# Attention probabilities turned by VectorE and SyncE's transfers, in place of TensorE

## The chip, the cores and the metric

The kernel runs on one core of a Trainium2 chip. The metric is the device time of one execution in microseconds (us). A core has TensorE (matrix products), VectorE, ScalarE and GpSimd, and SyncE, which here only issues transfers (DMA) and waits. Data lies in SBUF (128 partitions), products land in the eight banks of PSUM. In rows of the profile PE is a matmul, PEld its weight load, DVE VectorE, ACT ScalarE, POOL GpSimd, SPq SyncE's queue. L1409 is line 1409 of the kernel.

## The reference

Two different transformer blocks, one after the other, on a batch of 1, 512 tokens of width 1024, in f32. The first is attention over a sliding window (8 heads of 64, 2 key heads) beside a gated convolution, and a feed-forward part of width 2816. The second is two hybrid layers, each with a chunked attention (8 heads of 64) and a retention (4 heads of 128). What the change touches is the two attentions:

```python
def sliding_window_attention(q, k, v, sinks):      # first block: 128 queries, 256 keys
    scores = jnp.einsum("bnqhgd,bnkhd->bnhgqk", q, kw).astype(jnp.float32) * ATTN_SCALE
    scores = jnp.where(mask[None, :, None, None], scores, -jnp.inf)
    probs = jax.nn.softmax(jnp.concatenate([scores, sink], axis=-1), axis=-1)[..., :-1]
    out = jnp.einsum("bnhgqk,bnkhd->bnqhgd", probs.astype(v.dtype), vw)

def chunked_rel_attention(q, k, v, rel_bias):      # second block, both layers
    scores = jnp.einsum("bnqhd,bnkhd->bnhqk", qc, kb) * (dh ** -0.5)
    scores = jnp.where(valid, scores + bias[None, None], NEG_INF)
    p = jax.nn.softmax(scores, axis=-1)
    out = jnp.einsum("bnhqk,bnkhd->bnqhd", p, vb)
```

## The kernel before

**Units and projections.** All weights are taken in units of 1024 x 128. Two units are a panel, which SyncE loads into one of two slots of `raw` (two transfers of 512 KB) once `lo_ready` says that the units before it in this slot are split: panel n waits for 2n - 2 units. For unit u, ScalarE rounds it to `w_hi` and VectorE writes the rest, `w_lo`; both do so for unit u + 4 after TensorE's unit u. TensorE then takes 8 steps of three products (hi x hi, hi x lo, lo x hi, L608 to L610), 512 tokens wide, into one bank of `main`, and VectorE empties the bank with `apply_factor` (`bank_empty`). Numbers of units run through the whole program: 0 to 33 the first block's input, 50 to 93 the up projection, from 116 the second block's two layers with 40 units each.

**Attention in rounds and slots.** A round is two heads' scores for one or two blocks of 128 queries, 384 or 512 score columns in each of two banks (`half`). The first block has 8 rounds (four of them with 384 columns), each layer of the second has 10 (all 512). Rounds are threaded into the projection of other tiles in slots. Slot r lies after so many steps of the projection: in the first block in the middle of unit 20 + r, in the layers every 6 steps (`ATT2_SLOTS`). In slot r, in the order of each engine's queue:

- TensorE turns the probabilities of round r - 2 with transposes of 128 x 128 against `ident` (L687, six or eight a round) into `aux[2]` and `main[3]`, then makes the scores of round r (L698) in `aux[0]` and `aux[1]`, and in every second slot from r = 4 the value products of rounds r - 4 and r - 3 (`mix`, L675) in `aux[3]`.
- VectorE divides the exponentials of round r - 1 by their sums (`normalise`: reciprocal L1481, scaling L1486), takes scores plus table and maximum of round r out of the banks (`soften`, L1458), and reads `aux[3]` after value products.
- ScalarE copies the turned banks to SBUF (`copy_turned`, L1083) and takes the exponentials of round r (L1073), in the first block with one small exponential for each sink (L1070).

On VectorE and ScalarE a slot stands ahead of the unit's own work, `apply_factor` and split. All queues are in order, so work behind a slot waits for it. While the attention runs, the projection uses three banks of `main`. In the second block's layer 0 VectorE also scales `h` in units 6 to 13 of the layer, and from unit 17 on ScalarE, VectorE and GpSimd make the rotary tiles (`swapped`, `straight`).

**The start.** x arrives in four chunks and is turned on TensorE; the first four units are multiplied together, step by step as x comes. Their two panels are loaded by halves (4 of 8 rows of tiles each), and a unit's first product waits for `w_lo` of its first half. Twenty transposes of `ident` stand ahead (`warm_up`).

**The up projection's start.** In units 42 to 49 (out projection) ScalarE and VectorE split u + 4 ahead of adding the residual and rounding x. After unit 50 TensorE sums squares for the norm (`sum_norm`, L634), after unit 51 it spreads the factor.

Of the kernel before, what the change touches and what calls it, by code (L numbers as in the profile page):

```python
# [31 lines left out]
P = 128  # L32
# [41 lines left out]
ATT1 = 20  # L74
# [67 lines left out]
def two_blocks_kernel(  # L142
# [31 lines left out]
    diag_hi = keep("diag_hi", [P, NB, P], F32R)  # L174
    sum_sq_at = placed[0]
# [4 lines left out]
    squares = keep("squares", [P, 2, SEQ], F32)  # L180
    taps = keep("taps", [P, 132], F32)
# [42 lines left out]
    soft1_half = at("soft1_half", [P, 2, SEQ], F32, 88)  # L224
    turned1_pair = at("turned1_pair", [P, 2, 2, SEQ], F32, 80)
# [20 lines left out]
    soft2_pair = at("soft2_pair", [P, 2, 2, SEQ], F32, 80)  # L246
    turned2_half = at("turned2_half", [P, 2, SEQ], F32, 88)
# [19 lines left out]
    def soft1(r, half):  # L267
        return squares[:, half, :] if r % 2 else soft1_half[:, half, :]

    def soft2(r, half):  # L270
        return soft2_pair[:, r % 2, half, :]

    def turned1(r):
        return sum_sq if r % 3 == 2 else turned1_pair[:, r % 3, :, :]

    def turned2(r):
        return (turned2_half, squares, sum_sq)[r % 3]
# [17 lines left out]
    turned_banks = (aux[2], main[3])  # L295
# [32 lines left out]
    half_loaded = [sem("half_loaded0"), sem("half_loaded1")]  # L328
# [14 lines left out]
    bank_empty = sem("bank_empty")  # L343
    ident_ready = sem("ident_ready")
# [29 lines left out]
    probs_ready = sem("probs_ready")  # L374
    probs_turned = sem("probs_turned")
    turned_ready = sem("turned_ready")
# [96 lines left out]

    def in_rows(u):
        return u >= ROWS or u >= IN2 and (u - IN2) % LAYER_UNITS < VALUE_UNITS
# [14 lines left out]
    def _(sp):  # L490
        def panel(n, first, second):

            if n >= 2:
                sp.wait_ge(lo_ready, 2 * n - 2)
            load(n % 2, first, second)
# [30 lines left out]
        def first_panel(i, half):  # L526
            rows = tile_rows(w_in[0], 4 * half, 4, IN1_TILES[2 * i] * P, 256)
            sp.dma_start(raw[:, i, 4 * half:4 * half + 4, :], rows)\
                .then_inc(raw_loaded[i] if half else half_loaded[i], 16)
# [7 lines left out]
        x_chunk(2)  # L537
        x_chunk(3)
# [33 lines left out]
        def rows_panel(n, w, pair, column):  # L572
            sp.wait_ge(lo_ready, 2 * n - 2)
# [27 lines left out]
    def _(pe):  # L601
# [63 lines left out]
        def mix(n, spans, value, turned):  # L665

            pe.wait_ge(turned_ready, n + 1)
            if n >= 2:
                pe.wait_ge(mixed_read, n - n % 2)
            for step, (t, b, blocks, columns) in enumerate(spans):  # L670
                for j, kb in enumerate(blocks):
                    for half in range(2):
                        rows = slice(64 * half, 64 * half + 64)
                        column = columns.start + j * P
# [5 lines left out]
        def turn(n, r, spans, soft):  # L680

            if n >= 1:
                pe.wait_ge(turned_ready, n)
            for half in range(2):
                pe.wait_ge(probs_ready, 2 * n + half + 1)
                for j in range(spans[-1][3].stop // P):
                    done = pe.transpose(block_of(turned_banks[half], j), block_of(soft(r, half), j), ident[:])  # L687
                done.then_inc(probs_turned, 1)

        def score(n, spans, queries, keys):  # L690
            for t, b, blocks, columns in spans:
                query = queries[:, t, b * P:(b + 1) * P]
                key = keys(t)[:, blocks[0] * P:(blocks[-1] + 1) * P]
                for half in range(2):
                    if n >= 1 and columns.start == 0:
                        pe.wait_ge(peaked, 2 * n - 1 + half)
                    rows = slice(64 * half, 64 * half + 64)
                    done = pe.matmul(aux[half][:, columns], query[rows], key[rows], start=True, stop=True)  # L698
# [37 lines left out]
        def first_products(u, k):  # L736
            pe.wait_ge(x_ready, k + 1)
            if k == 0:
                pe.wait_ge(half_lo, u + 1)
# [1299 lines left out]
```

## Time and profile before

| | |
|---|---|
| time, median of 3 runs (lowest to highest) | 1218.19 us (1217.56 to 1218.64) |
| profiled execution: its own time / its span | 1218.59 us / 1216.7 us |
| TensorE busy (matmuls) | 1206.9 us, 5966 instructions |
| TensorE weight loads | 990.8 us |
| VectorE busy | 708.9 us, 1264 |
| ScalarE busy | 535.2 us, 948 |
| GpSimd busy | 90.5 us, 79 |
| granted clock, mean | 0.999 of full speed |
| moved by transfers | 114.05 MB, mean 94 GB/s |

Busy time of TensorE is from the start of a matmul to its modelled end, and neighbouring matmuls overlap. The span runs from the first to the last instruction of the profile; the execution's own time is 1.9 us longer. Durations come from this one execution.

### The profile page before, as it was taken

The page shows a single profiled execution, that of the slowest core. Times are in us where ns is not written, and L with a number is a line of the kernel's source. Part 1 is how long each engine was busy: PE and PEld are TensorE (multiplying, and loading weights), DVE is VectorE, ACT ScalarE, POOL GpSimd, SP SyncE. Part 2 cuts the span into 40 slices and gives each one's busy share as a digit, 9 for nine tenths or more (in the row PEclk, how much of TensorE's full clock was granted, in tenths as well). Part 3 has the DMA queues.
Part 4 walks back from the last instruction along what each step waited for, and adds up shares of the span by engine and source line. Part 5 has one row for each costly group of instructions (what it writes and reads, how often), then busy time and mean ns, then how long its engine had stood idle before and what let it go on. Part 6 is the DMA issues. An engine that isn't in the chain of part 4 may idle for free.

```text
span 1216.7 us, 16176 instructions
## 1 busy us (share of the span) xinstructions
PE 1206.9 (99%) x5966; PEld 990.8 (81%) x5966; DVE 708.9 (58%) x1264; ACT 535.2 (44%) x948; POOL 90.5 (7%) x79
## 2 busy tenths in 40 slices
PE   8999999999999999999999999999999999999997
PEld 7888788888888888888888887788888887788886
DVE  5555665564577777775642546665555335665654
ACT  4522563444444344442242424554654325454653
POOL 3000000002100000000010200033002000043000
PEclk9999999999999999999999999999999999999999
DMA  6333222332233223322233432222223521222121
GB/s 213 106 104 104 70 70 70 104 102 82 94 103 103 77 96 103 103 103 89 94 104 104 177 101 69 71 69 70 70 69 104 173 76 64 70 69 70 70 87 70
DMA packets 98202, 114.05 MB, mean 94 GB/s; under 512 B 3801, under 2 KB 82875, under 8 KB 98011
## 3 DMA queue, kind: packets, MB, share of 16 engines
q1 hardware_dynamic: 95755, 107.69, 27.0%
q10 hardware_dynamic: 2384, 5.51, 1.2%
q8 instruction: 41, 0.67, 0.2%
q14 instruction: 22, 0.18, 0.0%
HBM read 111.05 MB, written 2.14 MB: 93 GB/s over the span
## 4 chain that ended last, share of the span: by engine, by line
PE 97%; DVE 1%; DMA 1%; ACT 1%; issue 0%; POOL 0%; SPq 0%; ACTq 0%; DVEq 0%; POOLq 0%
PE main L608 23%; PE main L610 23%; PE main L609 23%; PE aux L608 3%; PE aux L610 3%; PE aux L609 3%; PE main L926 2%; PE main L928 2%; PE main L927 2%; PE aux L698 2%; PE aux L675 2%; PE aux L687 1%; PE main L687 1%; DMA raw<-in_w_in_dram 1%; PE main L993 1%; PE main L992 1%
## 5 line engine op out<-in xcount | busy, mean ns | idle before, releaser
L1409 DVE TENSOR_TENSOR w_lo<-raw,w_hi 128x1024 fp32r<-128x1024 f32 x192 | 243.6, 1270 | 266.3 <-ACT w_hi L1035 262.2
L608 PE MATMUL main<-x_hi,w_hi 128*128 128x512 f32 x984 | 392.1, 398 | 1.4 <-DVE w_lo L1496 1.4
L610 PE MATMUL main<-x_hi,w_lo 128*128 128x512 f32 x984 | 383.7, 390 | 0.0
L609 PE MATMUL main<-x_lo,w_hi 128*128 128x512 f32 x984 | 383.6, 390 | 0.0
L1035 ACT ACTIVATE w_hi<-raw 128x1024 fp32r<-128x1024 f32 x192 | 202.4, 1055 | 262.6 <-PE main L610 161.2
L608 PEld LDWEIGHTS main<-x_hi,w_hi 128*128 128x128 f32 x984 | 184.8, 188 | 50.6 <-issue 14.3
L610 PEld LDWEIGHTS main<-x_hi,w_lo 128*128 128x128 f32 x984 | 184.7, 188 | 39.6
L609 PEld LDWEIGHTS main<-x_lo,w_hi 128*128 128x128 f32 x984 | 185.0, 188 | 35.8
L1073 ACT ACTIVATE soft_pair<-soft_pair,neg_peak 128x128 f32<-128x128 f32 (+2 forms) x64 | 35.3, 553 | 56.3 <-DVE neg_peak L1465 56.3
L1446 DVE TENSOR_TENSOR up_in<-main,factor 128x512 f32<-128x512 f32 x44 | 30.4, 690 | 37.8 <-PE main L610 34.8
L926 PE MATMUL main<-w_hi,x_hi 128*128 128x512 f32 x128 | 50.5, 394 | 0.0
L928 PE MATMUL main<-w_lo,x_hi 128*128 128x512 f32 x128 | 50.0, 390 | 0.0
L927 PE MATMUL main<-w_hi,x_lo 128*128 128x512 f32 x128 | 49.9, 390 | 0.0
L1980 POOL COPY sum_sq<-squares 128x512 f32<-128x512 f32 x4 | 2.7, 670 | 618.4 <-ACT squares L1052 618.4
L1983 POOL TENSOR_TENSOR sum_sq<-sum_sq,squares 128x512 f32<-128x512 f32 x28 | 37.7, 1345 | 116.1 <-ACT squares L1052 115.4
L2001 POOL TENSOR_TENSOR swapped_pair<-swapped_pair,sin_t 128x512 f32<-128x512 f32 x16 | 24.4, 1528 | 256.7 <-ACT swapped_pair L1331 256.7
L1205 ACT ACTIVATE g_hi<-squares 128x512 f32 (+1 forms) x22 | 13.9, 633 | 65.1 <-DVE squares L1654 65.1
L608 PE MATMUL aux<-g_hi,w_hi 128*128 128x512 f32 x88 | 34.2, 389 | 0.0
L609 PE MATMUL aux<-g_lo,w_hi 128*128 128x512 f32 x88 | 34.2, 389 | 0.0
L610 PE MATMUL aux<-g_hi,w_lo 128*128 128x512 f32 x88 | 34.2, 389 | 0.0
L608 PE MATMUL main<-g_hi,w_hi 128*128 128x512 f32 x88 | 34.2, 389 | 0.0
L609 PE MATMUL main<-g_lo,w_hi 128*128 128x512 f32 x88 | 34.2, 389 | 0.0
(281 smaller groups left out, 1810.7 us busy)
## 6 DMA issues: line engine op xcount, KB each, us to landing
raw<-in_w_in_dram SPq DMA_DIRECT2D x98, 512.0 KB, 4.4
raw<-in_w_up_dram SPq DMA_DIRECT2D x44, 512.0 KB, 3.9
raw<-in_w_out_dram SPq DMA_DIRECT2D x24, 512.0 KB, 4.1
raw<-in_w_down_dram SPq DMA_DIRECT2D x22, 512.0 KB, 4.1
rel<-band_rows ACTq DMA_DIRECT2D x2, 2048.0 KB, 9.7
x_rows<-in_x_dram SPq DMA_DIRECT2D x4, 512.0 KB, 8.5
raw<-in_w_attn_branch_dram SPq DMA_DIRECT2D x4, 512.0 KB, 3.4
raw<-in_w_conv_branch_dram SPq DMA_DIRECT2D x4, 512.0 KB, 4.3
```

The source lines that it names most:

```text
L608: pe.matmul(bank, hi, right_hi[j], start=first and j == 0, stop=False)
L609: pe.matmul(bank, hi, right_lo[j], start=False, stop=False)
L610: done = pe.matmul(bank, lo, right_hi[j], start=False, stop=last and j == len(rows) - 1)
L926: pe.matmul(bank, x, hi, start=k == 0, stop=False)
L927: pe.matmul(bank, rest, hi, start=False, stop=False)
L928: return pe.matmul(bank, x, lo, start=False, stop=k == KT - 1)
L1035: act.activation(w_hi[:, u % 4, :, :], raw_unit(u), ACT.Copy).then_inc(hi_ready, 1)
L1073: done = act.activation(block, block, ACT.Exp, bias=neg_peak[which], accum_out=total[which])
L1409: dve.tensor_tensor(w_lo[:, u % 4, :, :], raw_unit(u), w_hi[:, u % 4, :, :].bitcast(F32), ALU.subtract).then_inc(lo_ready, 1)
L1446: dve.tensor_tensor(target, all_banks[main_bank(u)][:], factor[:], ALU.mult).then_inc(bank_empty, 1)
L1983: pool.tensor_tensor(sum_sq[:, 0, :], sum_sq[:, 0, :], tile, ALU.add)\
L2001: steps.then(pool.tensor_tensor(swapped(n), swapped(n), sin_t[:], ALU.mult))
```

## The change

**Attention.** TensorE's transposes (`turn`) and ScalarE's copies (`copy_turned`) go. VectorE transposes each round's probabilities by blocks of 32 x 32 into `blocks_turned`, one instruction for each half, and 16 transfers on SyncE's queue move the blocks of two rounds to where the whole is turned (each 32 partitions x 2 rounds x 256 columns, 64 KB). `normalise` moves from VectorE to ScalarE; VectorE keeps the reciprocal (`find_shares`). For the sinks VectorE subtracts the maxima for a round in one instruction and ScalarE takes one exponential. Work of two rounds now shares a slot: scores in even slots r for rounds r and r + 1, shares and normalising in slot r + 1, turning in slot r + 2, value products in slot r + 4. Two pairs of banks alternate for scores, so that `aux[2]` and `main[3]` hold scores too. `ATT1_SLOTS` and `ATT2_SLOTS` give the new places in steps: from unit 19.5 with 18 steps for two slots, and from 11.5 of each layer with 13 steps for two slots (6 more from slot 4). A move stands in SyncE's queue ahead of the first panel n for which the unit of its slot r + 2 is below 2n - 6. In a layer ScalarE waits ahead of the first rotary tile for `mixed`, GpSimd ahead of the fifth for the last `probs_turned`, since buffers share space.

**The start.** The first panels are loaded and split in pieces of 2, 2 and 4 rows. Step 0 of the four units goes two units at a time, product by product, each with a wait for its own operand. Five products of `mean` and seven transposes of `ident` replace most of the warm-up.

**The up projection.** The splits of units 52 and 53 go behind the residual and the rounding of x, the sum of the norm and the spreading go two steps into units 51 and 52.

```diff
+ATT1_SLOTS = [156 + 18 * (r // 2) + 10 * (r % 2) for r in range(len(ROUNDS1) + 3)]
-ATT2_SLOTS = [92 + 6 * r for r in range(len(ROUNDS2) + 3)]
+ATT2_SLOTS = [92 + 13 * (r // 2) + 8 * (r % 2) + (6 if r >= 4 else 0) for r in range(len(ROUNDS2) + 3)]
-ATT1 = 20
+ATT1 = 19
...
+    def rounds_scored(r, rounds):
+        return (r, r + 1) if r % 2 == 0 and r < len(rounds) else ()
+    def rounds_turned(r, rounds):
+        return (r - 2, r - 1) if r % 2 == 0 and 2 <= r < len(rounds) + 2 else ()
...
+    def round_banks(n):
+        return (aux[2], main[3]) if n % 2 else (aux[0], aux[1])
...
+        def move_blocks(n, turned):
+            sp.wait_ge(probs_turned, 2 * n + 4)
+            if n >= 4:
+                sp.wait_ge(mixed, n - 2)
+            for a in range(4):
+                for b in range(4):
+                    sp.dma_start(turned[32 * b:32 * b + 32, :, 256 * a:256 * a + 256],
+                                 blocks_turned[32 * a:32 * a + 32, :, b, :])\
+                        .then_inc(turned_ready[n // 2 % 2], 16)
+
+        def moves_before(n):
+            while moves and moves[0][0] < 2 * n - 6:
+                unit, r, turned = moves.pop(0)
+                move_blocks(r, turned)
...
         def mix(n, spans, value, turned):
-            pe.wait_ge(turned_ready, n + 1)
+            groups = turned[:, n % 2, :].rearrange("p (a s) -> p a s", a=4)
+            pe.wait_ge(turned_ready[n // 2 % 2], turned_count(n))
...
-                                         turned[:, half, column:column + P],
+                                         groups[:, :, at:at + 32],
...
+        def first_step(u):
+            hi, lo = w_hi[:, u % 4, 0, :], w_lo[:, u % 4, 0, :]
+            pe.wait_ge(x_hi_ready, 1)
+            pe.wait_ge(half_hi, u + 1)
+            pe.matmul(main[u][:], hi, x_hi[:, 0, :], start=True, stop=False)
+            yield
+            pe.wait_ge(x_ready, 1)
+            pe.matmul(main[u][:], hi, x_lo[:, 0, :], start=False, stop=False)
+            yield
+            pe.wait_ge(half_lo, u + 1)
+            pe.matmul(main[u][:], lo, x_hi[:, 0, :], start=False, stop=False)
+            yield
...
         for u in range(UP, UP + 4):
-            project(u, 1, wait=u == UP)
-            if u == UP:
-                sum_norm(2 * KT)
-            if u == UP + 1:
-                spread_factor(1)
+            def between(k, u=u):
+                if k == 2 and u == UP + 1:
+                    sum_norm(2 * KT)
+                if k == 2 and u == UP + 2:
+                    spread_factor(1)
+            project(u, 1, between, wait=u == UP)
...
+        def normalise(n, r, spans, soft):
+            act.wait_ge(shares_ready, n + 1)
             for half in range(2):
-                act.wait_ge(probs_turned, 2 * n + half + 1)
-                done = act.activation(turned[:, half, 0:width], turned_banks[half][:, 0:width], ACT.Copy)
-            done.then_inc(turned_ready, 1)
+                for step, (t, b, blocks, columns) in enumerate(spans):
+                    block = soft(r, half)[:, columns]
+                    done = act.activation(block, block, ACT.Copy, scale=share[:, n % 2, half, step:step + 1])
+                done.then_inc(probs_ready, 1)
...
+        def attention_slot(r, first, rounds, soft, sinks):
+            for m in rounds_scored(r, rounds):
+                exps(first + m, m, rounds[m], soft, sinks)
+            for m in rounds_scored(r - 1, rounds):
+                normalise(first + m, m, rounds[m], soft)
...
+        def turn(n, r, spans, soft):
+            if n >= 2:
+                before = n - n % 2 - 2
+                dve.wait_ge(turned_ready[before // 2 % 2], turned_count(before))
...
             for half in range(2):
+                dve.wait_ge(probs_ready, 2 * n + half + 1)
+                places = blocks_turned[:, r % 2, :, P * half:P * half + width // 4]
+                dve.transpose(places.rearrange("p b (k i) -> p k b i", i=32),
+                              soft(r, half)[:, 0:width].rearrange("p (k b j) -> p k b j", b=4, j=32))\
+                    .then_inc(probs_turned, 1)
...
         def slot1(r):
+            for m in rounds_scored(r - 1, rounds1):
+                find_shares(m, rounds1[m], True)
+            for m in rounds_turned(r, rounds1):
+                turn(m, m, rounds1[m], soft1)
+            for m in rounds_scored(r, rounds1):
+                soften(m, m, rounds1[m], lambda t, b, half: window[:, 0 if b else P:256], 0.125,
                        lambda t, half: sink_cols[:, 2 * t + half:2 * t + half + 1], soft1)
+                subtract_from_sinks(m, rounds1[m])
             for m in rounds_mixed(r, rounds1):
                 read_mixed(m, mixed_tile(q1, ROUNDS1[m]))
...
+                    if i == 17:
+                        act.wait_ge(mixed, len(ROUNDS1) + len(ROUNDS2) * layer + 4)
...
+                if n % 8 == 4:
+                    pool.wait_ge(probs_turned, 2 * (len(ROUNDS1) + len(ROUNDS2) * (layer + 1)))
```

## Rows read from the trace of the kernel before

**Rows 1.** The page, part 1: busy us, share of the span, instructions of each engine

```profile
PE 1206.9 (99%) x5966; PEld 990.8 (81%) x5966; DVE 708.9 (58%) x1264; ACT 535.2 (44%) x948; POOL 90.5 (7%) x79
```

**Rows 2.** TensorE's waits: us in total, times, longest us

```profile
PE main L608 <- DVE w_lo L1496: 1.4, 1, 1.4
PE aux L634 <- POOL sum_sq L1983: 0.2, 1, 0.2
```

**Rows 3.** Busy time by window: PE, PEld, VectorE, ScalarE, GpSimd; clock, DMA share, GB/s

```profile
736.00:826.00 90.00, 90.00 (x565) 69.91 (x564) 57.26 (x165) 45.89 (x106) 13.33 (x9) 1.00 0.18 59
```

**Rows 4.** TensorE's timeline: start us, us, instruction, at slots with scores and turning

```profile
126.34 0.93 PE L698 MATMUL aux<-k_twice,q 64*128 64x128 f32 x8
...
741.39 0.39 PE L609 MATMUL main<-x_lo,w_hi 128*128 128x512 f32 x1
741.61 0.39 PE L610 MATMUL main<-x_hi,w_lo 128*128 128x512 f32 x1
741.93 1.13 PE L698 MATMUL aux<-k,q 64*128 64x512 f32 x4
...
743.33 0.39 PE L609 MATMUL main<-x_lo,w_hi 128*128 128x512 f32 x1
...
753.25 0.39 PE L610 MATMUL main<-x_hi,w_lo 128*128 128x512 f32 x1
...
755.85 0.39 PE L609 MATMUL main<-x_lo,w_hi 128*128 128x512 f32 x1
```

**Rows 5.** The chain that ended last: start us, us, scores and value products

```profile
742.00 1.06 PE aux L698 x4
...
761.83 1.90 PE aux L675 x32
```

**Rows 6.** Groups of TensorE: busy us, mean ns of one, idle before

```profile
L675 PE MATMUL aux<-sum_sq,v 128*64 128x128 f32 x96 | 6.5, 277 | 0.0
```

**Rows 7.** TensorE's timeline at the start of the kernel

```profile
7.77 0.47 PE L608 MATMUL main<-x_hi,w_hi 128*128 128x512 f32 x1
...
10.80 0.47 PE L608 MATMUL main<-x_hi,w_hi 128*128 128x512 f32 x1 [1.43 <-DVE w_lo L1496]
```

**Rows 8.** ScalarE's timeline at the start of the kernel

```profile
9.30 1.15 ACT L1095 ACTIVATE w_hi<-raw 128x512 fp32r<-128x512 f32 x2 [1.54 <-DMA raw<-in_w_in_dram]
```

**Rows 9.** Groups of VectorE, shapes apart

```profile
L1458 DVE CUSTOM_DVE_ANT_0 soft_pair<-aux,rel 128x512 f32<-128x512 f32 x16 | 10.4, 686 | 1.4 <-PE aux L698 1.4
...
L1486 DVE TENSOR_SCALAR soft_pair<-soft_pair,share 128x512 f32<-128x512 f32 x16 | 7.1, 484 | 0.3
```

**Rows 10.** Groups of ScalarE, shapes apart

```profile
L1039 ACT ACTIVATE x_hi<-h,cols 128x512 fp32r<-128x512 f32 x16 | 11.6, 725 | 31.8 <-DVE h L1624 31.8
```

**Rows 11.** SyncE's timeline, small loads at the start

```profile
10.68 0.36 SPq L513 DMA_DIRECT2D vec_rows<-in_final_norm_dram  x1
...
13.40 0.42 SPq L523 DMA_DIRECT2D consts<-shape_constants  x1
```

**Rows 12.** Issues of transfers: count, KB each, median us from issue to landing

```profile
raw<-in_w_in_dram SPq DMA_DIRECT2D x98, 512.0 KB, 4.4
...
out_dram<-out_rows SPq DMA_DIRECT2D x8, 256.0 KB, 2.2
```

**Rows 13.** VectorE's timeline, first block and second block's layer 0

```profile
126.92 0.68 DVE L1446 TENSOR_TENSOR gates<-main,factor 128x512 f32<-128x512 f32 x1
...
755.99 0.17 DVE L1481 RECIPROCAL share<-total 128x4 f32<-128x4 f32 x1
...
761.89 1.23 DVE L1409 TENSOR_TENSOR w_lo<-raw,w_hi 128x1024 fp32r<-128x1024 f32 x1 [2.38 <-ACT w_hi L1035]
...
763.70 0.17 DVE L1481 RECIPROCAL share<-total 128x4 f32<-128x4 f32 x1
```

**Rows 14.** ScalarE's timeline, second block's layer 0

```profile
758.83 0.51 ACT L1073 ACTIVATE soft_pair<-soft_pair,neg_peak 128x256 f32<-128x256 f32 x1 [3.57 <-DVE neg_peak L1465]
...
760.82 1.04 ACT L1035 ACTIVATE w_hi<-raw 128x1024 fp32r<-128x1024 f32 x1
```

More of the change, by code:

```diff
@@ L490, in _ @@
     def _(sp):
+        moves = [(ATT1_SLOTS[r + 2] / 8, r, turned1(r // 2)) for r in range(0, len(ROUNDS1), 2)]
+        for layer in range(LAYERS):
+            moves += [(IN2 + LAYER_UNITS * layer + ATT2_SLOTS[r + 2] / 8,
+                       len(ROUNDS1) + len(ROUNDS2) * layer + r, turned2(r // 2)) for r in range(0, len(ROUNDS2), 2)]
+        def move_blocks(n, turned):
[11 more added lines that the diff above has]
+                move_blocks(r, turned)
         def panel(n, first, second):
+            moves_before(n)
             if n >= 2:
@@ L673, in mix @@
                         rows = slice(64 * half, 64 * half + 64)
-                        column = columns.start + j * P
+                        at = P * half + columns.start // 4 + 32 * j
                         done = pe.matmul(aux[3][rows, mixed_columns(n, step)], value(t, kb, half),
-                                         turned[:, half, column:column + P],
+                                         groups[:, :, at:at + 32],
                                          start=j == 0, stop=j == len(blocks) - 1)
             done.then_inc(mixed, 1)
[L680 to L688, printed above, removed]
         def score(n, spans, queries, keys):
@@ L694, in score, with attention_slot @@
                 for half in range(2):
-                    if n >= 1 and columns.start == 0:
-                        pe.wait_ge(peaked, 2 * n - 1 + half)
+                    if n >= 2 and columns.start == 0:
+                        pe.wait_ge(peaked, 2 * (n - 2) + half + 1)
                     rows = slice(64 * half, 64 * half + 64)
-                    done = pe.matmul(aux[half][:, columns], query[rows], key[rows], start=True, stop=True)
+                    done = pe.matmul(round_banks(n)[half][:, columns], query[rows], key[rows], start=True, stop=True)
                     if columns == spans[-1][3]:
                         done.then_inc(scored, 1)
-        def attention_slot(r, first, rounds, queries, keys, value, soft, turned):
-            if 2 <= r < len(rounds) + 2:
-                turn(first + r - 2, r - 2, rounds[r - 2], soft)
-            if r < len(rounds):
-                score(first + r, rounds[r], queries, keys)
+        def attention_slot(r, first, rounds, queries, keys, value, turned):
+            for m in rounds_scored(r, rounds):
+                score(first + m, rounds[m], queries, keys)
             for m in rounds_mixed(r, rounds):
-                mix(first + m, rounds[m], value, turned(m))
-        pe.wait_ge(ident_ready, 1)
+                mix(first + m, rounds[m], value, turned(m // 2))
+        pe.wait_ge(mean_ready, 1)
         def warm_up(times):
@@ L717, in warm_up @@
                 pe.transpose(main[3][:, 0:P], ident[:], ident[:])
-        warm_up(3)
+        for _ in range(5):
+            pe.matmul(main[3][:, 0:P], mean[:], mean[:], start=True, stop=True)
+        pe.wait_ge(ident_ready, 1)
         pe.wait_ge(mix_loaded, 16)
@@ L747, in _ @@
         turn_x(1)
-        warm_up(12)
-        for k in range(KT - 2):
+        warm_up(7)
+        for pair in ((0, 1), (2, 3)):
+            for _ in zip(*[first_step(u) for u in pair]):
+                pass
+        turn_x(2)
+        for k in range(1, KT - 2):
             for u in range(FIRST_UNITS):
                 first_products(u, k)
-                if u == (3 if k == 0 else 1):
+                if u == 1:
                     turn_x(k + 2)
@@ L844, in slot2 @@
                 for t in range(4):
-                    if r < len(ROUNDS2) and t in [step[0] for step in ROUNDS2[r]]:
+                    if t in [step[0] for m in rounds_scored(r, ROUNDS2) for step in ROUNDS2[m]]:
                         pe.wait_ge(bank_empty, emptied(u0 + KEY_UNITS[t]))
@@ L1598, in _ @@
                 convolve(t, t % 2)
-            if u - ATT1 in (4, 6, 8, 10):
-                attn_rest((u - ATT1 - 4) // 2)
+            for t in range(4):
+                if 8 * u < ATT1_SLOTS[2 * t + 4] <= 8 * u + 8:
+                    attn_rest(t)
         def merged_rest(m):
```

207 lines of the change are left out of this document (117 added, 90 removed).

## The prediction

> **What bounds the kernel now.** I read the page first. TensorE is busy for 1206.9 of 1216.7 us [rows 1]. The view of TensorE's waits names only short ones, 1.4 us for the first split weights and 0.2 us for a sum on GpSimd [rows 2]. So a microsecond taken out of TensorE's queue is a microsecond of the end, as long as nothing comes late to TensorE. The rest is about that condition: in the attention windows VectorE is busy for 57.3 of 90 us and ScalarE for 45.9 [rows 3], and I walked the timelines of both, and of SyncE, to see whether they can follow.
>
> **What leaves TensorE.** In its timeline products follow each other every 0.22 to 0.23 us: a step (three products) is 0.68 us, a unit of 24 products 5.44. A slot with scores alone takes 743.33 - 741.61 = 1.72 us, one with turning and scores 755.85 - 753.25 = 2.60 [rows 4]. Turning a round of 512 columns costs 0.88 us, one of 384 (six transposes for eight) 0.66. There are 24 and 4 of them: 21.1 + 2.6 = 23.8 us. The scores are 1.06 us [rows 5], so entering and leaving a slot costs 1.72 - 0.455 - 1.06 = 0.2 us. TensorE enters 6 + 7 + 7 slots in place of 11 + 13 + 13: 17 x 0.2 = 3.4 us. The scores and value products themselves stay, 1.90 us for the 32 value products of two rounds [rows 5]. Their moving operand is now four runs of 32 columns. No row has that; between nothing and twice the 0.06 us of one such product (432 of them, 26 us) I take nothing, as the nearest row, the same product with its 128 columns in one run (277 ns from start to end) [rows 6], gives no sign that the reading limits it.
>
> *First products.* Those of the first two units start at 7.77 us, those of the next two wait until 10.80 for the second panel, whose load ends at 9.30 [rows 7, 8]. With two of eight rows in the first pieces and step 0 of each unit by itself, I expect the first at about 6.6 and step 1 near 10.4 where it was near 12.6: 2 us, 1.2 if only half of each lateness goes, and 2.3 at most. The later sum of the norm takes away the 0.2 us of [rows 2] and about 0.1 beside it. Splits put later before the up projection are wanted two or three units afterwards: nothing.
>
> Without a new wait the sum is 23.8 + 3.4 + 2.0 + 0.3 = 29.5 us.
>
> **What may come late.** Four prices:
> - *A turn* of 512 columns on VectorE. The trace has none. A scaling in SBUF takes 0.48 us, a pass over PSUM 0.69, either with about 0.08 overlapped [rows 9]. Bounds 0.40 and twice 0.62; I take 0.62, since a transpose has to pass every element as the PSUM pass does. Two rounds: 2.5 us (2.2 in the first block).
> - *Normalising* on ScalarE: a scaled copy of 512 takes 0.725 with 0.1 overlapped [rows 10]; 1.25 for a round of one step, 1.6 for one of two, 2.85 for both. Bounds 2.0 and the 3.45 of the exponentials.
> - *The move* M, from turned to landed. Small loads leave SyncE every 0.39 us (10.68 to 13.40 is seven), a store lands 2.2 us after issue [rows 11, 12]. 15 x 0.39 + 1.8 = 7.6 us; bounds 6.5 and 10.
> - *The alternation* of the two engines. VectorE goes from share (755.99) to share (763.70) in 7.7 us; it waits for w_hi, because ScalarE does the exponentials first (758.83 to 760.82), and writes w_lo at 761.89 [rows 13, 14]. All of these stay in that order.
>
> The Trainium skill ("VectorE: DVE Perf Modes", section "The three transpose paths") gives 311 ns for a 128x128 turn in bf16. Four of them would be 1.24 us, by that estimate the result below would be 30 us later; no row here shows it.
>
> In the new order a unit with an even slot costs them turns 2.5, softening the first round 1.5, exponentials of both 3.45, w_hi 1.0, w_lo 1.15 = 9.6 us; one with an odd slot share 0.2, normalising 2.85, w_hi 1.0, w_lo 1.15 = 5.2. Together about 15, against TensorE's 13 x 0.68 + 2.12 + 1.90 + 0.2 = 13.1 from pair to pair. **VectorE and ScalarE, taking turns, become slower than TensorE in the attention**, though each has idle time.
>
> The walk in the second block, layer 0, from TensorE's start of unit 11. Unit 11: first scores there at 4.1, softened 7.0, exponentials 9.1, w_hi 10.1, w_lo 11.3, h scaled 12.0. Unit 12: share 12.2, normalised 15.1, w_hi 16.1, w_lo 17.3, h 18.0. Unit 13: turned 20.5, softened 23.7, exponentials 26.1, w_hi 27.1, w_lo 28.3, h 29.0. Unit 14: normalised 32.4, w_lo 34.6. Unit 15: turned 37.1. On in the same way, with the rotary passes from unit 17, the later pairs are turned at 52.2, 65.5 and 81.3. The five moves land at 28.1, 44.7, 59.8, 73.1, 88.9. TensorE, unstalled, reaches the value products at 31.3, 44.3, 57.4, 68.2, 79.1 (steps x 0.68 and its slots). It waits 0, 0.4, 2.0, 2.5 and 4.9, together 9.8 us. Layer 1 has no h scaling, is 2.1 earlier and waits 7.7.
>
> First block, from the start of unit 19 (118.2: the scores of unit 20.5 are at 126.34). VectorE is in a convolution until 126.92, 8.7 us [rows 4, 13]. It turns rounds 0 and 1 at 24.6, rounds 2 and 3 at 40.4. But the second move stands behind the load of panel 15 in SyncE's queue (its slot, 24.0, is not below 2 x 15 - 6), and that load waits for w_lo of unit 27, which VectorE writes at 48.3, after softening rounds 4 and 5. The move leaves at 49.3 and lands at 56.9; TensorE wants it at 26.25 units, 50.1: 6.8 us. The other three have 2 to 5 us in hand. Weight loads behind the moves are held by at most 3 us; they land after 4.4 [rows 12] and are wanted two units, over 10 us, later: nothing.
>
> Stalls together: 6.8 + 9.8 + 7.7 = 24.3 us. Against the profiled execution's own 1218.6: 1218.6 - 29.5 + 24.3 = 1213.4, and the median of the runs lies 0.4 below it: **1213.0 us**. The sum leans on M three times, and on the turn 48 times (20 in each layer, 8 before the second move): 0.1 us per turn is 4.8 us of the end.
>
> A stall may cost more than itself. The granted clock is at its full level (2.4 GHz) in each of the attention windows, with TensorE never idle there [rows 3]; I take no price, and each microsecond at half clock would lose half a microsecond. The Trainium skill ("TensorE: Matmul & The Clock Gate", section "HAM oscillation — how this bites in real kernels") says that a long enough standstill drops the clock to half; no row here shows one.
>
> **The rivals.**
> *Stalls small* (0.22). The moves have been given one slot of distance and lie beside other work. If a turn costs 0.45, or softening and exponentials overlap better than I walked, the stalls fall to 8 to 15 us. For it: 33 of 90 us of VectorE are idle [rows 3]. Against it: most of that idle time is the wait for w_hi. Time 1197 to 1205.
> *Slower: the turn is dear* (0.25). It is one price in one place, in the serial path ahead of softening, 48 times. The 5.2 us of gain are gone at 0.62 + 5.2/48 = 0.73 us, at 0.85 the time is 1224, at twice the price 1243. Output in runs of 32 set 256 apart could do it. The trace doesn't exclude it.
> *No change* (0.13). The stalls just eat the gain, 1215.7 to 1220.5: M near 9.3 us does that, or a clock that falls at the three longest stalls and loses about 1 us at each.
>
> **The numbers.** My forecast (stalls of 18 to 27 us) has 0.40 and its own range is 1206 to 1215.7. Within 0.2% (2.4 us, about what a measurement tells from no change) 0.13, slower 0.25, faster 0.40 + 0.22 = 0.62. About 0.1 lies below 1197 and 0.1 above 1226; that takes in a turn from 0.45 to 0.85 and M from 6.5 to 10.
>
> **What would show it.** Right: TensorE's busy time lower by some 27 us and no turning on it; TensorE waiting for transfers at the value products in all three attentions, longest at the last pair of each layer and the second of the first block; a turn near 0.69 us; 16 issues in about 6 us; product train from about 6.6 us. Wrong: hardly a wait there (the alternation is shorter than walked); waits at scores or projections for a bank or for w_lo (lateness hits elsewhere); value products more than 0.06 us apart; a clock below full.

## The result and the profile after

The changed kernel takes 1226.80 us (median of 4 runs, 1226.47 to 1227.39) against 1217.88 us in the runs of the kernel before that were timed beside it: ratio 1.0073, 95% interval 1.0061 to 1.0085. It is slower by 8.9 us. The forecast was 1213.0 us and faster, with a range of 1197 to 1226; the sign is wrong, and the time lies 0.8 us outside the range. The profiled execution took 1226.8 us, its span is 1225.0.

The page of the kernel after, parts 1 and 4 (busy time, chain of work):

```profile
PE 1186.3 (97%) x5752; PEld 976.7 (80%) x5752; DVE 710.1 (58%) x1237; ACT 543.2 (44%) x968; POOL 90.7 (7%) x79
...
PE 79%; ACT 5%; SPq 5%; DVE 5%; issue 3%; DMA 1%; DVEq 0%; POOL 0%; ACTq 0%; POOLq 0%
```

TensorE has 20.6 us less busy time than in [rows 1], yet the span is 8.3 us longer. SyncE's queue, which only issues transfers, is now 5% of the chain that ends last. The view of TensorE's waits, where [rows 2] had two short ones (a third of the kernel before, at its very start, is not among those rows; here the wait for `mean` stands in its place):

```profile
PE main L717 <- POOL ident L1961: 2.1, 1, 2.1
```

And of the kernel after:

```profile
PE aux L733 <- DMA both_sums<-blocks_turned: 14.0, 7, 3.7
PE aux L733 <- DMA late_gates<-blocks_turned: 7.6, 2, 7.4
PE aux L733 <- DMA rel_begin<-blocks_turned: 5.6, 2, 3.6
PE aux L733 <- DMA swapped_on<-blocks_turned: 3.7, 2, 2.1
PE main L766 <- POOL mean L2062: 1.0, 1, 1.0
PE aux L746 <- DVE k L1521: 0.6, 1, 0.6
```

30.9 us of waiting stand at one line, the value products, and all of it for moved blocks, in 13 of the 14 pairs of rounds. The second block's layer 0 on three timelines (start, length, engine, line, idle time before in brackets): VectorE's turns, SyncE's issues, TensorE's value products.

```profile
772.49 2.49 DVE L1579 STREAM_TRANSPOSE blocks_turned<-soft_pair 128x512 f32<-128x512 f32 x4
787.36 2.48 DVE L1579 STREAM_TRANSPOSE blocks_turned<-soft_pair 128x512 f32<-128x512 f32 x4
801.67 2.49 DVE L1579 STREAM_TRANSPOSE blocks_turned<-soft_pair 128x512 f32<-128x512 f32 x4 [2.40 <-DMA both_sums<-blocks_turned]
```

```profile
775.00 10.24 SPq L532 DMA_DIRECT2D swapped_on<-blocks_turned  x16
```

```profile
771.62 1.97 PE L733 MATMUL aux<-both_sums,v 128*64 128x128 f32 x32 [1.84 <-DMA both_sums<-blocks_turned]
786.68 1.97 PE L733 MATMUL aux<-swapped_on,v 128*64 128x128 f32 x32 [2.10 <-DMA swapped_on<-blocks_turned]
801.69 2.79 PE L733 MATMUL aux<-both_sums,v 128*64 128x128 f32 x32 [2.03 <-DMA both_sums<-blocks_turned]
816.25 3.63 PE L733 MATMUL aux<-rel_begin,v 128*64 128x128 f32 x32 [1.97 <-DMA rel_begin<-blocks_turned]
830.69 1.97 PE L733 MATMUL aux<-both_sums,v 128*64 128x128 f32 x32 [1.72 <-DMA both_sums<-blocks_turned]
```

Read one pair across them. The second is turned at 772.49 + 2.49 = 774.98, and its value products start at 786.68, 11.7 us later. Its 16 issues take 10.2 us, 0.64 each (those of the first pair 11.5), and a transfer lands 2.0 us after its issue. M, the time from turned to landed, is 11.7 to 13.1 us in the second block's ten pairs (mean 12.1), where the forecast had 7.6 and a bound of 10. It also closes a loop: there is one `blocks_turned`, so the turn at 801.67 had to wait 2.40 us until the blocks of the pair before had landed. A turn (2.5) and a move (11.8) are 14.3 us, more than TensorE takes for a pair: 13.1 in the forecast, 12.9 between the first two pairs of layer 0 in the run without moves below.

The windows (busy time of each engine, granted clock, DMA share, GB/s) over three stretches behind a wait:

```profile
802.70:807.00 4.30, 4.30 (x26) 3.53 (x23) 4.30 (x18) 2.11 (x7) 1.27 (x1) 0.61 0.70 232
816.20:819.80 3.60, 3.54 (x32) 3.26 (x32) 2.79 (x5) 0.43 (x1) 1.27 (x1) 0.53 0.52 164
...
1070.00:1080.00 10.00, 7.92 (x63) 6.10 (x60) 7.57 (x26) 6.56 (x17) 3.44 (x3) 1.00 0.55 165
```

In the first two the clock is at its lower level, 1.2 GHz, while TensorE works; the attentions have five such stretches, each of some 3.4 us of work at half speed. The one from 816 follows a standstill of 1.97 us, while one of 2.08 us in layer 1, at 1073.69, is followed by none (third row). The Trainium skill ("TensorE: Matmul & The Clock Gate", section "HAM oscillation — how this bites in real kernels") says that a long enough standstill drops the clock to half. The trace agrees in that all five stretches stand behind a wait, the longest of 7.37 us; the length of the wait alone doesn't tell which ones, as the pair of 1.97 and 2.08 us shows.

### The profile page after: what moved, and what is told of

Read it like the earlier page. It is cut to its first block, busy times and chain, and to the rows that moved or that the text cites. A ratio compares the mean times of both kernels' runs of the same rounds, so it can differ in the third digit from the quotient of the medians.

```text
span 1225.0 us, 15972 instructions
## 1 busy us (share of the span) xinstructions
PE 1186.3 (97%) x5752; PEld 976.7 (80%) x5752; DVE 710.1 (58%) x1237; ACT 543.2 (44%) x968; POOL 90.7 (7%) x79
## 4 chain that ended last, share of the span: by engine, by line
PE 79%; ACT 5%; SPq 5%; DVE 5%; issue 3%; DMA 1%; DVEq 0%; POOL 0%; ACTq 0%; POOLq 0%
PE main L665 19%; PE main L666 19%; PE main L667 19%; SPq L532 5%; PE aux L665 3%; PE aux L666 3%; PE aux L667 3%; PE main L992 2%; PE main L994 2%; PE main L993 2%; ACT soft_pair L1149 2%; ACT soft_pair L1136 2%; DVE blocks_turned L1579 2%; DVE soft_pair L1533 1%; ACT w_hi L1101 1%
## 5 line engine op out<-in xcount | busy, mean ns | idle before, releaser
L1136 ACT ACTIVATE soft_pair<-soft_pair,neg_peak 128x128 f32<-128x128 f32 (+2 forms) x96 | 50.2, 524 | 63.0 <-DVE neg_peak L1540 62.5
L1149 ACT ACTIVATE soft_pair<-soft_pair,share 128x128 f32<-128x128 f32 (+2 forms) x96 | 42.4, 522 | 21.0 <-DVE share L1565 20.8
L1579 DVE STREAM_TRANSPOSE blocks_turned<-soft_pair 128x512 f32<-128x512 f32 (+1 forms) x56 | 33.7, 660 | 9.9 <-DMA late_gates<-blocks_turned 5.1
```

The costliest lines, as they stand in the source:

```text
L1136: done = act.activation(block, block, ACT.Exp, bias=neg_peak[which], accum_out=total[which])
L1149: done = act.activation(block, block, ACT.Copy, scale=share[:, n % 2, half, step:step + 1])
L1579: dve.transpose(places.rearrange("p b (k i) -> p k b i", i=32), soft(r, half)[:, 0:width].rearrange("p (k b j) -> p k b j", b=4, j=32))\
```

## The experiments

The theory: 16 transfers at 0.65 us of issue each make a move cost 12 us; TensorE's lateness at the end of an attention is (time turned + M - time wanted), so each microsecond of M is one of the end in each of the three attentions. The rivals: the alternation of VectorE and ScalarE is too slow by itself; the bytes moved, not their number, set M; the fall of the clock makes the loss. A move in fewer than eight transfers was not tried.

| run | time, us | ratio to before (95%) |
|---|---|---|
| e4_direct | 1188.7 | 0.9764 (0.9749 to 0.9779) |
| e2_count8 | 1217.4 | 0.9996 (0.9987 to 1.0005) |
| e3_count32 | 1367.6 | 1.1235 (1.1218 to 1.1252) |
| e1_order | 1222.0 | 1.0038 (1.0024 to 1.0052) |
| e5_start | 1216.4 | 0.9987 (0.9978 to 0.9996) |
| e6_filler | 1228.8 | 1.0092 (1.0076 to 1.0107) |
| e12_count8_filler | 1215.9 | 0.9984 (0.9975 to 0.9993) |
| e7_two_queues | 1210.8 | 0.9945 (0.9932 to 0.9959) |
| e9_later | 1207.1 | 0.9913 (0.9899 to 0.9926) |
| e8_two_later | 1195.8 | 0.9820 (0.9807 to 0.9834) |
| e10_best1 | 1193.1 | 0.9803 (0.9790 to 0.9817) |
| e11_best2 | 1195.2 | 0.9817 (0.9804 to 0.9831) |

The intervals are each kernel's against the kernel before, timed beside it; they are 2 to 4 us wide, so between two of these runs a difference of 2 us or less is not clear of noise.

**No moves.** VectorE's transposes write `turned` itself, and `mix` waits for them (part of the edit):

```diff
-            pe.wait_ge(turned_ready[n // 2 % 2], turned_count(n))
+            pe.wait_ge(probs_turned, 2 * n + 2)
```

> No moves: VectorE turns the blocks straight into the buffers that the value products read, and TensorE waits for the turn alone. Blocks stay in their 32 partitions, so the values mixed are not the reference's. This is the change with a move that costs nothing, and it holds the two rivals apart: if the alternation of VectorE and ScalarE (or the turn of 0.68 us) makes TensorE wait by itself, waits stay at the value products of the last pairs of each layer (turned at 80.8 us of the block, wanted at 79.1: 1.7 us there, and nothing elsewhere). If the moves alone make them, no wait is left but that 1.7 us in each layer, the clock stays at full level throughout, and the whole 29.5 us of work taken from TensorE come out: 1188 to 1193.

Measured: 1188.7 us, and this view of TensorE's waits:

```profile
PE aux L731 <- DVE q L1545: 1.3, 2, 0.9
PE main L764 <- POOL mean L2060: 1.0, 1, 1.0
PE aux L744 <- DVE k L1519: 0.6, 1, 0.6
PE main L663 <- DVE gates L1519: 0.2, 1, 0.2
```

The first row is two waits at the last two pairs of layer 0, for VectorE's reading of the products before (`q`), which stands behind turning or softening in its queue; the third is one at a score; the second is the start's. I had expected 1.7 us at the last pair of each layer: layer 1 has none. So the alternation with its 56 turns on VectorE costs TensorE 1.9 us in all. Falls: the alternation as the cause. The loss, 1226.8 - 1188.7 = 38.1 us, is the moves'.

**Half as many transfers, and twice as many**, with the same bytes:

```diff
-            for a in range(4):
+            for a in range(2):
                 for b in range(4):
-                    sp.dma_start(turned[32 * b:32 * b + 32, :, 256 * a:256 * a + 256],
-                                 blocks_turned[32 * a:32 * a + 32, :, b, :])\
+                    sp.dma_start(turned[64 * (1 - a):64 * (1 - a) + 64, :, 256 * b:256 * b + 256],
+                                 blocks_turned[64 * a:64 * a + 64, :, b, :])\
```

> Every move carries the same 1 MB in 8 transfers of 64 partitions in place of 16 of 32; half of the blocks land in other places, so the values mixed are not the reference's. If the price of a move is SyncE's 0.65 us per issued transfer, its issues take 5.2 us in place of 10.3, a move lands 7.2 us after the turn in place of 12.2, and of the waits for moves (31.5 us in the changed kernel) nearly all but the one behind panel 15 go: layer 0 waits near 0, 0, 0, 0 and 0 to 1 us, the first block near 0 and 3 to 5; with most stretches at half clock gone the time is 1197 to 1204. If the price goes with the bytes (64 KB per transfer at a rate), the issues take 10 us as before and the time stays at 1225 to 1228.

> The same bytes in 32 transfers of half the columns; the values are those of the changed kernel. By count a move is 21 us of issues and lands 23 us after the turn, 10.5 later than now: each of the 14 moves is late by 8 to 12 us more, less what the later turn of the next pair gives back; if TensorE simply waits longer at each it is 100 to 145 us more, and SyncE is busy with issues for longer than a pair of rounds takes TensorE (13 us), so that the moves queue up behind each other and hold the weight loads too: 1320 to 1420. By bytes the time stays at 1225 to 1228.

SyncE in the run with 8, second pair of layer 0, and then TensorE's value products in the first block and late in layer 0:

```profile
773.57 5.25 SPq L532 DMA_DIRECT2D swapped_on<-blocks_turned  x8
```

```profile
175.84 3.26 PE L733 MATMUL aux<-late_gates,v_rows 128*64 128x128 f32 x28 [10.15 <-DMA late_gates<-blocks_turned]
192.60 1.75 PE L733 MATMUL aux<-both_sums,v_rows 128*64 128x128 f32 x28
...
824.72 1.97 PE L733 MATMUL aux<-both_sums,v 128*64 128x128 f32 x32 [3.16 <-DMA both_sums<-blocks_turned]
```

An issue of 128 KB takes 0.65 us like one of 64 KB, and in the run with 32 transfers one of 32 KB takes 0.64: the price goes by the number. M is 6.9 to 8.4 us in the ten pairs of the layers with 8 (mean some 7.5), and 22 us with 32, whose time, 1367.6, is in the middle of what the count gives. Falls: the bytes. But the time with 8 is 1217.4, not the 1197 to 1204 that I expected: I had counted on the waits going, and with M close to the 7.6 of the forecast 24.2 us of them are left. That the forecast had 24.3 is partly luck: the layers wait 14.0 us, forecast 17.5, and the first block's second pair 10.15, forecast 6.8. That move leaves SyncE at 165.9, right behind the two halves of panel 15, and lands 9.9 us later. Its transfers take 5.0 us (median) from issue to landing; three moves issued 1.2 to 1.5 us behind a load take 3.4 to 3.5, the other ten 2.3 to 2.5.

How late TensorE is can be had from its timelines alone: from where it reaches the first value products of an attention to the start of the last ones (us).

| | first block | layer 0 | layer 1 | sum | less no moves | median less no moves |
|---|---|---|---|---|---|---|
| no moves | 44.7 | 49.2 | 47.8 | 141.7 | | |
| 8 transfers | 57.5 | 56.5 | 55.0 | 169.0 | 27.3 | 28.7 |
| the change, 16 | 58.9 | 60.9 | 59.5 | 179.3 | 37.6 | 38.1 |
| 16, order changed | 53.7 | 60.9 | 59.7 | 174.3 | 32.6 | 33.2 |

The last two columns agree within 1.4 us: the three attentions hold the loss. From 8 to 16 transfers M grows by some 4.6 us and the end by 4.4 or 4.5 us in each layer, as the theory has it, but by 1.4 only in the first block.

**The order of the second move.**

```diff
-            while moves and moves[0][0] < 2 * n - 6:
+            while moves and moves[0][0] <= 2 * n - 6:
```

> The second move stands ahead of the load of panel 15 in SyncE's queue, in place of behind it; nothing else is changed. With the move behind the panel, rounds 2 and 3 leave 9 us after they were turned and TensorE waits 7.4 us at 178.0, and the clock is at half for 3.5 us after it. If the place in the queue is what makes that wait, rounds 2 and 3 leave at once when they are turned (some 9 us sooner), the 7.4 us wait is gone, and with it a stretch at half clock worth 1.7 us; panel 15 is loaded up to 10 us later and is wanted later still. Forecast: 7 to 9 us less than the changed kernel's 1226.8, so 1218 to 1220. Rival: the wait is only moved, because rounds 4 and 5 or the loads behind the moves come late by as much; then 1224 to 1227.

Measured: 1222.0, 4.8 us less, where I expected 7 to 9. The 7.37 us wait is gone (the second pair starts at 170.11 without one, in place of 178.03), and the first block ends 5.2 us sooner by the table. What is missing went to the third pair, which now waits 2.29 us and has a stretch at half clock behind it: the rival in part.

**The start alone**, in the kernel before, with the up projection's later sum. It leaves out the five products of `mean`: ahead of x it turns the identity as the kernel before does.

> The kernel before with the start of the change alone (first panels in three pieces, step 0 of each unit by itself, shorter warm-up, mean ahead of the identity) and the later sum of the norm in the up projection. TensorE still turns the probabilities; attention is that of before, with no move and no stall. In the changed kernel the third units' step 1 starts 1.85 us sooner and the 0.2 us wait for a sum is gone. If this part is worth what it shows there: 1215.6 to 1216.2, 1.9 to 2.1 us below the kernel before. Rival: the lead is lost again further on, at splits that come in the same order as before, so that only up to 0.6 us stays.

Measured: 1.4 us less, 0.5 to 2.7 by the interval, below the 1.9 to 2.1 that I expected. Step 1 starts at 11.18 us, against 12.62 in the kernel before and 10.78 in the change. Most of the lead stays; the interval just reaches the rival's 0.6, and what the products of `mean` add was not tested.

**The clock.** TensorE turns the identity ahead of the waits:

```diff
-            pe.wait_ge(turned_ready[n // 2 % 2], turned_count(n))
             if n >= 2:
                 pe.wait_ge(mixed_read, n - n % 2)
+            for _ in range({0: 31, 2: 62, 4: 0, 6: 0, 8: 14, 10: 17, 12: 16, 14: 16, ...}.get(n, 0)):
+                pe.transpose(aux[3][:, mixed_columns(n, 0)], ident[:], ident[:])
+            pe.wait_ge(turned_ready[n // 2 % 2], turned_count(n))
```

> The changed kernel, in which TensorE turns the identity into an unused bank ahead of 12 of the 14 waits for a move, for about as long as each wait lasts; nothing else waits for it. The waits stay, but TensorE doesn't stand still in them. If the standstills are what drops the clock to half (five stretches of some 3.4 us, worth 1.7 us each), the granted clock stays full and the time falls by 6 to 9 us, to 1218 to 1221. Rival: the clock's falls have another cause, or the waits grow by the filling; then the time stays at 1226 or more.

Over 118 to 216, 740 to 845 and 1015 to 1115 us, the three attentions, the granted clock is 1.00, 0.98 and 1.00, where it was 0.95, 0.97 and 0.98; the time is not less (1228.8). Layer 0's value products in this run:

```profile
771.36 1.97 PE L735 MATMUL aux<-both_sums,v 128*64 128x128 f32 x32
786.61 1.97 PE L735 MATMUL aux<-swapped_on,v 128*64 128x128 f32 x32 [0.28 <-DMA swapped_on<-blocks_turned]
801.75 1.97 PE L735 MATMUL aux<-both_sums,v 128*64 128x128 f32 x32 [0.28 <-DMA both_sums<-blocks_turned]
816.18 1.97 PE L735 MATMUL aux<-rel_begin,v 128*64 128x128 f32 x32 [1.64 <-DMA rel_begin<-blocks_turned]
830.75 3.18 PE L735 MATMUL aux<-both_sums,v 128*64 128x128 f32 x32 [1.97 <-DMA both_sums<-blocks_turned]
```

They start within 0.3 us of where they start in the changed kernel, and so do the last ones of the first block (208.25 against 208.26). The blocks come when SyncE has moved them; a TensorE that works faster in between waits longer: 12.0 us of waits are left and 251 turns of 0.113 us (62 in 6.99) stand before them. That is 40.3 us, where the changed kernel waited 30.9 and lost half of 17 us at half clock. The 2 us more come behind the last products of layer 0 (half clock there after all) and in layer 1. The rival of this run holds: in the changed kernel the half clock costs next to nothing of its own.

With 8 transfers only one turn waits for a move, that of the first block's third pair (2.9 us; my expectation has none), and half clock should cost there:

> The run with 8 transfers per move (half of the blocks in other places, so the values mixed are not the reference's), with TensorE turning the identity into an unused bank ahead of its six waits. There VectorE's turn never waits for a move, so TensorE is late by the standstill and by the half clock after it: after the 10.2 us wait the next value products come 16.8 us later where they come 14.2 later at full clock. If a fall of the clock costs where the pace is not set by the loop of turning and moving: 2.6 us in the first block and 0 to 2 us elsewhere, 1213 to 1215, against 1217.4 without the filling. Rival: as in the other filled run, the next wait takes up what the clock gave, and the time stays at 1216.5 or more.

In the profiled execution the next value products come 14.2 us after the second pair's (176.03 to 190.20) in place of 16.8, and it took 1213.8 us against 1217.8. But the runs spread from 1213.8 to 1219.2, the medians are 1.5 us apart and the intervals of the two ratios overlap. That 2.6 us of the first block went with the half clock is shown by the timeline; how much of it is left at the end stays open (taken as in the table, the three attentions are 2.0 us shorter together).

**Issued by two queues.** On top of the order, GpSimd issues the half with a = 2 and 3, with semaphores of its own:

```diff
+            for a in (2, 3):
+                for b in range(4):
+                    pool.dma_start(turned[32 * b:32 * b + 32, :, 256 * a:256 * a + 256], ...
...
+                for pair in {0: (0, 1, 2), 2: (3,), 4: (4,)}.get(n % 8, ()):
+                    move_blocks(len(ROUNDS1) + len(ROUNDS2) * layer + 2 * pair, turned2(pair))
```

> The second move ahead of panel 15, and each move's 16 transfers issued half by SyncE and half by GpSimd (which is idle there); the values are those of the changed kernel. If a move costs what one queue takes to issue it (0.65 us per transfer on SyncE), and GpSimd issues as fast, a move lands 7.2 us after the turn, as with 8 transfers on one queue; the waits are those of that run without the 10.2 us behind panel 15, 14 us, and the time is 1203 to 1207. Rival: an issue by GpSimd costs 1.2 us or more, then a move lands after 12 us as before and the time stays at 1222 or more; or the 16 transfers are limited by what moves them, with the same result.

Measured 1210.8: 16.0 us below the change, and 3.8 above the upper end of what I expected. The third pair of layer 0 is turned at 779.9 and its products start at 786.7 after a wait, so M is 6.7 us there. GpSimd at the fourth pair:

```profile
793.65 1.29 POOL L2124 TENSOR_TENSOR swapped_pair<-swapped_pair,sin_t 128x512 f32<-128x512 f32 x1 [3.27 <-ACT swapped_pair L1408]
797.70 1.27 POOL L2131 TENSOR_TENSOR rq<-straight_pair,swapped_pair 128x512 f32<-128x512 f32 x1 [2.77 <-DVE straight_pair L1944]
798.91 4.26 POOL L2101 DMA_DIRECT2D rel_begin<-blocks_turned  x8
```

Eight issues take 4.3 us there, less than on SyncE (5.1). But the pair was turned at 793.0, and its issues stand behind a rotary pass that I had put ahead of them; TensorE waited 6.9 us there and 6.7 us in layer 1. It is the fault of the second move in the change again, on another queue.

**Value products later.** The last three pairs of each layer are mixed in the odd slot behind the one of the change, 8 steps later (and `turned` takes other buffers for two of them, not shown):

```diff
-        return (r - 4, r - 3) if r % 2 == 0 and 4 <= r < len(rounds) + 3 else ()
+        pairs = (4, 6, 9, 11, 13) if len(rounds) == len(ROUNDS2) else (4, 6, 8, 10)
+        return (2 * pairs.index(r), 2 * pairs.index(r) + 1) if r in pairs else ()
```

With moves from SyncE alone:

> The second move ahead of panel 15, all 16 transfers from SyncE as in the change (a move still costs 12 us), and the value products of the last three pairs of each layer 8 steps (5.4 us) later. With the order alone, TensorE is 13 us late at the last pair of a layer. If its lateness is the time of the turn plus the move less the time at which the products are wanted, 5.4 us of it go in each layer and 7 to 8 us stay: 1222.0 - 10.8 = 1211, 1209 to 1213. Rival: the loop of turning and moving (a turn waits until the move before has landed, 14.7 us a pair against TensorE's 13.1) sets the pace whatever the distance; then only 0 to 3 us go.

With two queues:

> As the run with two queues, and in the second block the value products of the last three pairs of rounds stand in the slot that has no scores, 8 steps (5.4 us) after the one in which they stand now (other buffers for two of the pairs, one slot more per layer). The waits left for those pairs were 1.3 to 3.7 us with moves of 7 us, all below 5.4. If TensorE's lateness there comes from the time between turn and wanted product alone, all of them go, no stretch at half clock is left, and the time is 1190 to 1195. Rival: the alternation of VectorE and ScalarE (a pair each 14 to 15 us, against TensorE's 13.1) sets the pace, and the wait appears at the scores or at the split weights in their place: 1200 or more.

Measured 1207.1 and 1195.8: either 14.9 us below the same kernel without it. The expected 10.8 with one queue was too little: the waits at the value products fell from 25.1 to 14.1 us, and of three stretches at half clock in the layers one is left. How the 14.9 divides between waits and clock was not tested. The loop of 14.3 us did not set the pace over the five pairs of a layer. With two queues the time is 0.8 us above what I expected; 2.4 us of waits for moves that GpSimd issued late are left.

**The version that beats both.** The moves ahead of the rotary pass in GpSimd's queue, and, in the second of these, the first block's third pair later as well:

> As the run with two queues and later value products, with GpSimd's fourth and fifth moves each one rotary pass further ahead in its queue. The 2.4 us that TensorE waited there for moves issued late by GpSimd go: 1193 to 1194.5. Rival: the rotary pass that now stands behind the move is late and holds ScalarE's swaps and so the split weights; then 1196 or more.

> As the run before it, and in the first block the value products of the third pair of rounds 10 steps (6.8 us) later, in the slot without scores. The 3.0 us wait there goes, and nothing takes its place: 1190.5 to 1192.5. Rival: the fourth pair's value products, still in their own slot and wanted 0.6 us late before, wait 3 us in its place: as the run before it.

The first takes 1193.1 us, 24.6 below the kernel before (ratio 0.9803). In both layers its value products wait for nothing; the view of waits has, besides the short ones that all these runs share, only the first block's two:

```profile
PE aux L736 <- DMA both_sums<-blocks_turned: 2.8, 1, 2.8
PE aux L736 <- DMA late_gates<-blocks_turned: 2.0, 1, 2.0
```

The second takes 1195.2, where I expected 1190.5 to 1192.5: the third pair's wait is gone, and the fourth, still in its own slot, waits 4.9 us in its place. The rival of that expectation holds; the intervals of the two kernels overlap, so which of them is faster stays open.

## Why the prediction was wrong

**The step that failed** is "15 x 0.39 + 1.8 = 7.6 us; bounds 6.5 and 10", the size of the move. I took the spacing of an issue from the small loads of [rows 11]; these transfers leave every 0.65 us, so 15 x 0.65 + 2.0 = 11.8; the mean over the ten pairs is 12.1. Its weight, "the sum leans on M three times", would make 3 x (12.1 - 7.6) = 13.5 us, 1226.5 in all. That this comes so near is chance: the run with 8 transfers, whose M is the forecast's, takes 1217.4, so M is 9.4 of the 13.8 us that I was off, once in each layer and hardly in the first block. The other 4.4 lie mainly in the first block, which was mis-sized even with M right (below). With M right the change would have been no gain either. Twice the row would have been the honest upper bound, since no row of before moves SBUF to SBUF in pieces.

The other steps, one by one:

- *TensorE's 29.5 us.* Right: without moves the kernel gains 28.9 us with 1.9 us of waiting left, 30.8. The page of that run has TensorE at 1176.8 us, 30.1 below [rows 1]. Inside it, the start (without the products of `mean`) and the sum of the norm gave 1.4 (forecast 2.3). The first products came at 7.59 us in the changed kernel, not at 6.6, step 1 at 10.78 (forecast 10.4). Value products still take 1.97 us for 32 against 1.90 in [rows 5]; the four runs of 32 columns cost 1 us in all at most (14 pairs x 0.07).
- *The turn.* 0.68 us each, forecast 0.69 from start to end, from the pass over PSUM of [rows 9]. This group answers to it (engine, shapes, count, busy us and mean ns):

```profile
L1579 DVE STREAM_TRANSPOSE blocks_turned<-soft_pair 128x512 f32<-128x512 f32 x48 | 29.9, 677 | 4.8 <-DMA both_sums<-blocks_turned 4.8
L1579 DVE STREAM_TRANSPOSE blocks_turned<-soft_pair 128x384 f32<-128x384 f32 x8 | 4.1, 555 | 5.1 <-DMA late_gates<-blocks_turned 5.1
```

  The estimate from the Trainium skill's figure for a 128x128 turn in bf16 ("VectorE: DVE Perf Modes", section "The three transpose paths"), 1.24 us, is almost twice what the trace shows for this f32 form.
- *The alternation.* Right in its times: pairs turned at 36.8, 51.7, 66.0 and 80.8 us in layer 0, forecast 37.1, 52.2, 65.5 and 81.3. The 66.0 holds the wait of 2.40 us for blocks not yet moved, which I had not forecast; the run without moves has 64.7 and 80.0 for the last two. That it makes VectorE and ScalarE the slower side is right, too, but a distance of one slot pair covers it all but 1.9 us.
- *The first block.* The second move leaves at 49.6 from the start of unit 19, forecast 49.3, and stands behind panel 15 as walked. With M as forecast (8 transfers) the block is 12.8 us late, not 6.8: 2.3 us because the blocks land 9.9 us after they leave and not 7.6, right behind the panel's bytes, 2.6 from the half clock behind the standstill, 0.9 from TensorE arriving sooner. The layers are 8.6 and 7.2 us late in that run, forecast 9.8 and 7.7.
- *The clock.* It fell five times in the attentions, and I priced it at nothing. In the changed kernel the price is next to nothing, for a reason that I did not give: the next blocks come at their time anyway.
- *The rivals.* Slower came true, but not by the turn. "No change" named the true cause, M, and stopped at 9.3 us, where it had only to go on. With M at 12 by its own rule, three times M, it ends where the kernel ended, by the same chance.

Corrected: 1218.6 - 29.5 + 38.9 (13.0 and 11.7 late in the layers against 47.9 unstalled and 47.8, 14.2 in the first block) = 1228.0; with the 30.8 that TensorE really lost in place of 29.5 it is 1226.7, against the profiled 1226.8. The 38.9 are read from the changed kernel's own trace, so this shows that the account is complete, not that it could have been foretold.

## What to carry to other kernels

When a change hands work to transfers, price the issuing engine first: number of transfers times its interval, taken from transfers of the same kind or, where the trace has none, with a bound at least twice the nearest row; bytes came second here by far. Compare turned-plus-moved with wanted for the last pair, not for the first, and make up what is missing by distance (an odd slot 5.4 us later was worth 15 us) or by a second queue. In each queue that issues, look at what stands just ahead of a move whose time is near, and do not count stalls and half clock twice where the following wait takes up both.

## What the hardware showed that I had not expected

Transfers from SBUF to SBUF leave SyncE every 0.64 to 0.65 us whether they carry 32, 64 or 128 KB; eight by GpSimd take 4.3 us. The DMA engines are by no means full meanwhile: over the three stretches named above they are busy for 0.37, 0.38 and 0.40 of the time in the changed kernel and move 108 to 116 GB/s. Eight transfers of 128 KB issued right behind two loads of 512 KB landed 5.0 us after their issue (median), against 2.3 to 2.5 where no load had left for 2.8 us or more. And the clock fell to 1.2 GHz behind a standstill of 1.97 us, though not behind each one of that length.
